# First model of a two-model kernel: each weight panel fetched by two transfers of half its columns, on the same queue

## The reference, cut to what matters

```
h = x @ w_in[l]                                   # 1024 x 10016: branch inputs, gates, merge gates
y_rwkv, y_mla, y_conv, y_mem = four branches of h # time mixing, latent attention, convolution, memory attention
proj   = einsum('bsnc,ncd->bsnd', branches, w_o_branch[l])
gates  = sigmoid(merge + b_gate[l])
merged = sum(gates * proj, over the four branches)
x      = layer_norm(alpha * x + merged @ w_out[l])
```

## Time and profile before

| | us |
|---|---|
| median of three executions | 3212.06 |
| the three | 3212.91, 3199.82, 3212.06 |
| the profiled execution, its own time | 3211.31 |
| its span, first to last instruction | 3209.4 |
| part of the span that is the first model | about 1272 |
| PE busy in the first 1272 us | 1175.45 |

### The profile page before, as it was taken

The page is one execution under the profiler, slowest core; times in us unless marked ns, Lnnn a source line. Parts: engine busy times, 40 slices in busy tenths (PEclk is TensorE's granted clock), DMA queues, the critical chain, the costliest instruction groups (busy, mean ns, idle before and its releaser), DMA issues.

```text
span 3209.4 us, 41520 instructions
## 1 busy us (share of the span) xinstructions
PE 2938.6 (92%) x16084; PEld 2428.2 (76%) x16084; DVE 1136.6 (35%) x1705; ACT 703.9 (22%) x1331; POOL 1254.3 (39%) x531
## 2 busy tenths in 40 slices
PE   8999899999998996899989897999979999788798
PEld 7976688689766873788868676888868888676696
DVE  2822843246328333300341453001340023424437
ACT  3432211144322121211121232111131111213211
POOL 4700000067000000566655303556645666552586
PEclk9999999999999998999999968999989999899899
DMA  6555532454465232322222102222213222220353
GB/s 227 182 186 188 217 119 79 171 176 171 171 236 193 97 132 105 106 93 103 92 92 73 59 1 73 79 103 93 92 66 105 91 93 103 73 98 27 113 175 131
DMA packets 67458, 383.87 MB, mean 120 GB/s; under 512 B 19072, under 2 KB 20736, under 8 KB 21888
## 3 DMA queue, kind: packets, MB, share of 16 engines
q1 hardware_dynamic: 66464, 379.19, 33.1%
q10 hardware_dynamic: 864, 2.84, 0.2%
HBM read 380.96 MB, written 1.05 MB: 119 GB/s over the span
## 4 chain that ended last, share of the span: by engine, by line
issue 30%; POOL 10%; POOLq 9%; PE 5%; DMA 3%; DVE 1%; SPq 1%; ACT 1%; DVEq 0%; ACTq 0%
POOL m_ws L1653 9%; POOLq L1652 7%; DMA m_ring<-in_panels 3%; PE m_bank L1760 2%; POOLq L1665 1%; SPq L1606 1%; POOL m_ws L1671 1%; POOLq L1670 1%; PE m_bank L1912 0%; PE m_bank L1697 0%; DVE m_ws L2154 0%; PE m_bank L1699 0%; PE m_bank L1698 0%; PE m_bank L1890 0%; PE m_bank L1877 0%
## 5 line engine op out<-in xcount | busy, mean ns | idle before, releaser
L1697 PE MATMUL m_bank<-m_aT,m_ws 128*128 128x512 f32 (+1 forms) x1664 | 603.5, 363 | 21.9 <-POOL m_ws L1653 6.3
L1698 PE MATMUL m_bank<-m_aT_low,m_ws 128*128 128x512 f32 (+1 forms) x1664 | 601.0, 361 | 0.0
L1699 PE MATMUL m_bank<-m_aT,m_ws 128*128 128x512 f32 (+1 forms) x1664 | 601.0, 361 | 0.0
L1653 POOL TENSOR_TENSOR m_ws<-m_ring,m_ws 128x2048 fp32r<-128x2048 f32 x127 | 592.7, 4667 | 18.7
L342 POOL TENSOR_TENSOR m_ws<-m_ring,m_ws 128x2048 fp32r<-128x2048 f32 x48 | 221.0, 4613 | 574.9 <-ACT m_ws L814 574.9
L1760 PE MATMUL m_bank<-m_ws,m_hs 128*128 128x512 f32 x1848 | 422.6, 390 | 3.4 <-issue 1.7
L1760 PEld LDWEIGHTS m_bank<-m_ws,m_hs 128*128 128x128 f32 x1848 | 346.1, 188 | 79.3 <-issue 7.1
L1697 PEld LDWEIGHTS m_bank<-m_aT,m_ws 128*128 128x128 f32 x1664 | 315.2, 189 | 73.9 <-issue 18.0
L1664 POOL TENSOR_TENSOR m_small<-m_small 128x1 f32<-128x1 f32 x158 | 32.5, 206 | 828.5 <-PE m_bank L1699 455.1
L1698 PEld LDWEIGHTS m_bank<-m_aT_low,m_ws 128*128 128x128 f32 x1664 | 315.4, 190 | 47.3
L1699 PEld LDWEIGHTS m_bank<-m_aT,m_ws 128*128 128x128 f32 x1664 | 315.3, 189 | 47.1
(11 more groups left out here) (355 smaller groups left out, 4004.6 us busy)
## 6 DMA issues: line engine op xcount, KB each, us to landing
m_ring<-in_panels SPq DMA_DIRECT2D x352, 1024.0 KB, 4.9
m_bias<-in_rpb SPq DMA_DIRECT2D x48, 64.0 KB, 2.3
m_hT<-in_ln_rows ACTq DMA_DIRECT2D x2, 1024.0 KB, 7.7
m_con<-in_con SPq DMA_DIRECT2D x1, 1408.0 KB, 11.8
m_memT<-in_memT SPq DMA_DIRECT2D x1, 1024.0 KB, 5.8
x_tok<-in_x SPq DMA_DIRECT2D x1, 1024.0 KB, 14.6
m_ctx_tok<-in_ctx SPq DMA_DIRECT2D x1, 1024.0 KB, 5.0
out<-x_tok SPq DMA_DIRECT2D x1, 1024.0 KB, 4.0
```

Source lines behind the costliest of these rows:

```text
L1653: nc.gpsimd.tensor_tensor(ws[:, p, 1, :], ring[:, p, :], ws[:, p, 0, :].bitcast(F32), ALU.subtract)\
L1697: mm(out, w, a, start=start, stop=False)
L1698: mm(out, w, a_low, start=False, stop=False)
L1699: return mm(out, w_low, a, start=False, stop=stop)
```

## The change

The slot is cut into two halves of 1024 columns (4 KB per partition). Each panel is fetched by two transfers, one for each half, issued one behind the other on SyncE's queue, without a wait between them. Both add 16 to the slot's semaphore, so readers wait for multiples of 32. Nothing is read before both halves are there. The order of panels, the waits of the queue and everything on the compute engines stay.

```diff
+        halves = (slice(0, PAN // 2), slice(PAN // 2, PAN))
+
         @block.sync
         def _(sp):
             sp.dma_start(memT[:, :, :], io["memT"]).then_inc(s["mem_in"], 16)
-            sp.dma_start(ring[:, 0, :], io["panels1"][0, :, :]).then_inc(slot[0], 16)
-            sp.dma_start(ring[:, 1, :], io["panels1"][1, :, :]).then_inc(slot[1], 16)
+            for p in range(2):
+                for h in halves:
+                    sp.dma_start(ring[:, p, h], io["panels1"][p, :, h]).then_inc(slot[p], 16)
             ...
-            sp.dma_start(ring[:, 2, :], io["panels1"][2, :, :]).then_inc(slot[2], 16)
-            sp.dma_start(ring[:, 3, :], io["panels1"][3, :, :]).then_inc(slot[3], 16)
+            for p in range(2, RING):
+                for h in halves:
+                    sp.dma_start(ring[:, p, h], io["panels1"][p, :, h]).then_inc(slot[p], 16)
             sp.dma_start(cin[:, :, :].rearrange("p k s -> p (k s)"), io["c"]).then_inc(s["c_in"], 16)
             with sp.Fori(1, DEPTH * PANELS1 // RING) as g:
                 for p in range(RING):
 
                     sp.wait_ge(s["panel_used"], (g - 1) * RING + p + 1)
-                    sp.dma_start(ring[:, p, :], io["panels1"][bass.ds(g * RING + p, 1), :, :]
-                                 .rearrange("o p n -> p (o n)")).then_inc(slot[p], 16)
+                    for h in halves:
+                        sp.dma_start(ring[:, p, h], io["panels1"][bass.ds(g * RING + p, 1), :, h]
+                                     .rearrange("o p n -> p (o n)")).then_inc(slot[p], 16)
...
-                    pe.wait_ge(slot[n % RING], (l * (PANELS1 // RING) + n // RING + 1) * 16)
+                    pe.wait_ge(slot[n % RING], (l * (PANELS1 // RING) + n // RING + 1) * 32)
...
-                    act.wait_ge(slot[n % RING], (l * (PANELS1 // RING) + n // RING + 1) * 16)
+                    act.wait_ge(slot[n % RING], (l * (PANELS1 // RING) + n // RING + 1) * 32)
```

## The result

Over 20 executions of each, the kernel before has a median of 3199.61 us (3187.57 to 3213.61) and the changed one of 3219.09 us (3199.99 to 3234.46). The ratio of the means is 1.0056, with a 95% interval of 1.0036 to 1.0075: the change costs 0.4 to 0.75%, 11 to 24 us. The measured median lies inside the range of the forecast, but the effect is not the one that was forecast: 2 us were expected, and 12 to 18 came.

What follows compares the result with a forecast made beforehand. PE was taken to bound the kernel, busy 92% of the span, with panel latency seen at 15 waits. 15 x 0.15 = 2.25 us on 3211.31 gave 3213.6 us, range 3199.82 to 3228.

Steps and rivals of the forecast that it cites:

- What bounds the kernel: PE is busy 92% of the span; its panel waits, about 35 us, mostly show transfer latency on an empty queue.
- Rows of half the length: Panel transfers with 4 KB rows in place of 8 KB: 0 to 0.2 us longer per panel, taken as 0.1.
- One more transfer: A second transfer per panel in the middle of a stream: 0.05 us for its start and end.
- The issue costs nothing: On SyncE's queue the second half, asked for 0.4 us later, is covered by 1.25 us of first-half data.
- c_in behind panel 3: Program-start input of 8 KB, landing 0.1 us behind panel 3; the source of the 0.05 us per extra transfer.
- The bias transfers: 64 KB transfers issued every 0.6 to 0.7 us, each landing after 2.3 us; taken to show that fixed time overlaps.
- the second issue counts: Rival: landing follows the second issue, each panel 0.4 + 0.15 us late, 8 us at 15 places, 3219.5 us; 11 in 100.
- The rival in which the halves don't overlap at all: Fixed part paid twice, empty-queue landing 6.9 us, 32 us at 15 places, 3243 us at least; 6 in 100.
- The count and the sum: PE's panel waits in the first model: 15 places, each later by 0.15 us, adding 2.25 us.
- The 15 places: Where PE waits for a panel: 12 gate waits, two of mod_rows and the program's first wait, about 35 us.
- The base of the sum: The profiled execution of the kernel before, 3211.31 us, to which 2.25 us were added.
- The page's rule: Skill page advising transfers of at least 1 MiB; two halves that don't overlap would add some 30 us at 15 places.

Runs made afterwards that it cites:

- the run with one transfer: Against the kernel before: each panel still one transfer, but of 256 rows of 4 KB, its halves apart in device memory; ratio 0.9992.
- the run with the small part last: The changed kernel with each panel cut unevenly, first 1792 columns, then 256, in place of equal halves; ratio to the kernel before 1.0009.
- the version with half waits: The changed kernel with a semaphore for each half; gate, branch and mod_rows start on the first half; ratio to the kernel before 0.9941.

## Why the prediction was right and wrong

*What bounds the kernel* was read rightly. PE waits for panels mainly behind mod_rows, the latency of a transfer on an empty queue is what it sees there, and the split projections hide theirs (1.0 when they alone are cut).

*Rows of half the length*, 0.1 us per panel, was right within its range of 0 to 0.2: 0.06 us on an empty queue and 0.05 in a full one, shown by the run with one transfer.

*One more transfer*, 0.05 us, is the term that was mis-sized, and with it "The issue costs nothing". The two together measure 0.47 - 0.06 = 0.41 us on an empty queue. The rows that I leaned on, c_in behind panel 3 and the inputs behind each other, are transfers in a queue full of earlier data, issued 12 us and more before their turn. For that case the term was right: in a full queue a panel in halves takes 2.53 us, no more than one transfer with the same rows. A second half behind only 1.25 us of data on an empty queue is another case, and the run with the small part last shows the difference: behind 2.2 us of data the cost is nearly gone. I had argued that the second half, issued 0.4 us after the first (0.52 in the trace), is in time for the end of the first, "provided that its own start-up runs beside the first's data". It does run beside it, with hardly a pause between the halves, and still eight of the 16 parts end 0.4 us later. The bias transfers showed that several can be under way at once, not that the engines lose nothing by it. The rival "the second issue counts" had the size, 0.55 us per panel, and not the reason, since the landing isn't tied to the second issue in the run with the small part last. The rival in which the halves don't overlap at all, 6.9 us, is out.

*The count and the sum.* The 15 places were to take 2.25 us. With 0.47 us each they would take 7 us, and the waits took 14.9. The rest is the late landings and the longer step: the gates' waits grew by 9.7 us at 12 places, 0.8 each, the two of mod_rows by 1.2 and 1.3 us, and waits came up at two new places of mod_rows (0.4 and 0.8 us) and one of branch. The 14.9 are of one execution, whose first model is 20.3 us longer; by the groups of executions, 12 to 13 us are usual. That a panel waits for the slowest of 16 engines wasn't in the forecast. That two transfers give more chances for one to be late would fit the 26 of 104 late landings, but no run tests it. What makes a single engine late is not settled by these runs.

*The clock* was left out. PE is busy for 6.9 us more for the same 7568 products of the stage. A gate behind a longer wait shows how. Before, after 2.52 us of waiting; then after the change, 3.17 us (PE in order of time):

```profile
296.74 7.17 PE L394 MATMUL m_bank<-m_xF,m_ring 128*128 128x256 f32 x32 [2.52 <-DMA m_ring<-in_panels]
```

```profile
298.94 8.86 PE L399 MATMUL m_bank<-m_xF,m_ring 128*128 128x256 f32 x32 [3.17 <-DMA m_ring<-in_panels]
```

The same products take 1.7 us longer. In the stretch of the second gate the granted clock is 0.81, in that of the first 1.00:

```profile
298.90:307.80 8.90, 8.86 (x34) 7.50 (x35) 0.00 (x0) 0.00 (x0) 0.00 (x0) 0.81 0.82 329
```

```profile
296.70:303.90 7.20, 7.17 (x34) 6.30 (x35) 0.00 (x0) 0.00 (x0) 0.00 (x0) 1.00 0.95 396
```

The clock has two levels, 2.4 GHz and 1.2 GHz; 0.81 is a mean of both: the trace has it at the lower one from 299.5 to 302.9 us. By the Trainium skill, page "TensorE: Matmul & The Clock Gate", section "What's actually happening", the array falls to the lower one when it has been idle; the row agrees, with the drop behind the longer wait. In the changed kernel's profile all five gates behind waits of 3.2 to 5.1 us take 8.6 to 9.9 us. Behind waits of about 2.5 us both happen: before, the gate at 919.4 us takes 8.86 us behind 2.51, and the one shown above 7.17 behind 2.52. But the 6.9 us are not a steady part of the cost: with only the other panels in halves PE's busy time is as before while the ratio is 1.0068, and with only the split projections in halves one execution shows 1179.73 us with gate waits of 22.6 us, hardly more than before. So longer waits for panels are shown to be the cause; how much the clock adds to them on average is argued from single executions.

*The absolute number.* The base of the sum, 3211.31 us, was an execution in the upper part of the kernel's spread. In 20 executions the median before is 3199.61. The base was so 11.7 us too high, and the effect of 2.25 us far too small; that the median of 3219.09 lies 5.5 us from the forecast of 3213.6 and inside its range is luck, since the two errors partly cancel. Against the median before, the forecast of 2.25 us would have been 3201.9.

*The page's rule.* The Trainium skill's advice in "DMA: Bandwidth & Descriptors", section "Measured (HBM→SBUF, 128 partitions, SWDGE, issued from GpSimd)", to make transfers at least 1 MiB had the sign right. The estimate from the formula of its section "Anatomy of one DMA" without overlap, 2 us more per panel, is four times the 0.47 us that were measured.

## What to carry to other kernels

A transfer that is cut in two on an empty queue can land later as a whole: by 0.47 us with two halves, by next to nothing with the small part behind 2.2 us of data, and hardly at all in a full queue. Judge that from a pair of transfers issued together on an empty queue, not from the middle of a full one. Cut a transfer only where the reader can begin on the first part, with a semaphore for each: the same cut then turned from a ratio of 1.0056 to one of 0.9941. And where PE waits for transfers, price a longer wait with the lower clock behind it in mind.

## What the runs showed of the hardware

- A panel moved as two transfers of 64 partitions (8 KB rows) lands in steps of 4.9 us in a queue, as one of 128 partitions in 2.5 us. All 16 parts signal in both, yet the rate is half.
- Twice as many rows of half the length in one transfer cost 0.05 to 0.06 us per MB.
- The second model, which no run here touches, takes either about 1937 us or about 1918 us. The window of the version with half waits shows the shorter one:

```profile
1258.60:3177.00 1918.40, 1739.77 (x8516) 1441.77 (x8516) 577.94 (x886) 368.43 (x796) 1034.14 (x479) 0.96 0.27 91
```

  It has the same 8516 products as in the earlier trace rows, which take 1739.77 us at 0.96 in place of 1763.11 at 0.95. So 19 us of the spread between executions of one kernel come with the granted clock of PE in the second model, as much as the change itself costs, and comparing two single profiles by their spans would have given anything from nothing to twice the effect. In the profiles shown here a mean clock of the whole execution of 0.962 and more goes with the shorter second model, and 0.956 and less with the longer one; only the run by partitions, with its long first model, has 0.956 and the shorter one.

  By that clock the 20 executions of the changed kernel are 8 of 3208.1 us in the mean (0.961 and more) and 12 of 3226.3; before, by their times, they are 14 of 3195.9 and 6 of 3212.9. The differences are 12.2 and 13.4 us. In three other sets of executions of the kernel before, the longer group came up in 11 of 22, 16 of 35 and 12 of 23, so its 6 of 20 here are at least in part chance. A comparison by stage leaves the second model out, but the first model differs between executions too: with only the other panels in halves its profile shows 9.7 us more, and the nine executions of its longer group are 13.6 us above those of the kernel before.
